# Output stages of a two-layer decoder trunk: turning activation rows by DMA transposes of f16 halves in place of TensorE transposes

## What is computed

```
h = RMSNorm(x) ; p = h @ w_in          # 3328 columns: heads of group A and of group B
A = sliding-window attention with sinks (8 query heads, 2 key heads, window 128)
B = retention with per-head decay (4 heads), per-head RMS norm
mixed = concat(silu(g_A) * A, silu(g_B) * B)
x = x + mixed @ w_out                  # 1024 x 1024
```

## Time and profile before

| | us |
|---|---|
| median of 3 runs | 2056.47 (2053.58 to 2058.32) |
| profiled execution, its own time | 2057.81 |
| span of that execution, first to last instruction | 2055.3 |
| O of layer 0, first to last matmul | 883.85 to 1093.5 |
| O of layer 1, first to last matmul | 1866.68 to 2050.9 |
| PE, DVE, ACT busy over the span | 93%, 71%, 38% |

### The profile page before, as it was taken

One profiled execution on the slowest core, in us unless ns is written; L12 is line 12 of the kernel. 1 busy time (PEld: TensorE's weight loads), 2 busy tenths in 40 slices (PEclk: granted clock), 3 DMA queues, 4 the chain that ended last, 5 costly groups with the idle time before them and its releaser, 6 DMA issues.

```text
span 2055.3 us, 38859 instructions
## 1 busy us (share of the span) xinstructions
PE 1915.4 (93%) x12808; PEld 1111.9 (54%) x12808; DVE 1451.5 (71%) x5064; ACT 782.3 (38%) x1977; POOL 67.7 (3%) x108
## 2 busy tenths in 40 slices
PE   2279999999999999999998999999999999999999
PEld 2246565555555555554554655565555555555454
DVE  6548999987665676668874799999766567666342
ACT  5634555552222223234653445555322221223121
POOL 4000000010000000030001000000000000000000
PEclk9589999999999999999999999999999999999999
DMA  8631000021100210053333000001210021002442
GB/s 277 235 106 28 16 16 10 15 74 60 31 10 10 96 60 10 13 190 115 131 124 123 28 15 11 15 13 34 80 50 10 13 96 60 10 10 91 144 153 92
DMA packets 68283, 137.52 MB, mean 67 GB/s; under 512 B 9808, under 2 KB 40720, under 8 KB 67888
## 3 DMA queue, kind: packets, MB, share of 16 engines
q1 hardware_dynamic: 58464, 100.76, 14.3%
q0 software_dynamic: 9728, 35.66, 5.1%
HBM read 97.27 MB, written 49.68 MB: 71 GB/s over the span
## 4 chain that ended last, share of the span: by engine, by line
PE 40%; DVE 12%; issue 2%; ACT 2%; DMA 1%; DVEq 0%; SPq 0%; ACTq 0%
PE PA L461 16%; PE PB L461 15%; DVE r L997 2%; DVE r L973 1%; DVE mix L1037 1%; DVE w_mx L830 1%; PE OB L626 1%; PE S L607 1%; PE TK L596 1%; ACT r L1541 1%; PE S L642 1%; PE X L648 1%; PE OB L633 1%; PE X L559 1%; PE TK L648 1%
## 5 line engine op out<-in xcount | busy, mean ns | idle before, releaser
L461 PE MATMUL PA<-w_a,hT 128*128 128x512 f16 (+1 forms) x1920 | 403.1, 360 | 8.1 <-DVE land L951 8.1
L461 PE MATMUL PB<-w_a,hT 128*128 128x512 f16 (+1 forms) x1920 | 402.1, 359 | 0.0
L461 PEld LDWEIGHTS PA<-w_a,hT 128*128 (+1 forms) x1920 | 185.3, 99 | 181.3 <-DVE land L951 9.0
L461 PEld LDWEIGHTS PB<-w_a,hT 128*128 (+1 forms) x1920 | 184.6, 98 | 178.1 <-issue 10.5
L1541 ACT ACTIVATE r<-r,nm,unqk 128x256 f32<-128x256 f32 x256 | 150.5, 589 | 116.2 <-DVE sd L1005 116.2
L1599 ACT ACTIVATE r<-OB 128x128 f32<-128x128 f32 (+1 forms) x136 | 36.3, 272 | 386.5 <-PE S L642 360.1
L461 PE MATMUL PA<-w_b,hT 128*128 128x512 f16 x768 | 179.3, 384 | 0.0
L461 PE MATMUL PA<-w_b,r 128*128 128x512 f16 x768 | 177.1, 382 | 1.9 <-DVE r L1191 1.6
L461 PE MATMUL PB<-w_b,hT 128*128 128x512 f16 x768 | 176.3, 379 | 0.0
L461 PE MATMUL PB<-w_b,r 128*128 128x512 f16 x768 | 173.8, 379 | 0.0
L1086 DVE TENSOR_TENSOR r<-S,t_dec 128x256 f32<-128x256 f32 x64 | 27.1, 424 | 153.6 <-PE S L607 153.5
(11 more groups left out here) (239 smaller groups left out, 3036.1 us busy)
## 6 DMA issues: line engine op xcount, KB each, us to landing
out<-r SPq DMA_DIRECT2D x40, 512.0 KB, 2.6
r<-mixed SPq DMA_DIRECT2D x32, 512.0 KB, 4.5
r<-out SPq DMA_DIRECT2D x32, 512.0 KB, 3.5
r<-in_x_prompt SPq DMA_DIRECT2D x16, 512.0 KB, 6.1
w_b<-in_w_in POOLq DMA_DIRECT2D x16, 512.0 KB, 9.0
mixed<-mix SPq DMA_DIRECT2D x32, 256.0 KB, 2.0
w_a<-in_w_in POOLq DMA_DIRECT2D x16, 512.0 KB, 8.1
mixed<-mix SPq DMA_DIRECT2D x64, 128.0 KB, 1.8
```

Of the source, the lines that this page charges most:

```text
L461: last = nc.tensor.matmul(out[0:s.rows, 0:n], lhs, w16(ph, k, p, wpart), start=(k == 0 and part == 0 and wpart == 0), stop=(k == KT - 1 an ...
```

## The change

In O, the rows stay with tokens on partitions until they are f16 halves, and the halves are turned by a DMA. ACT `o_mhi` now writes hi = f16(mixed row times `minv`) to `mh`, one instruction; DVE `o_mlo` writes lo = (row times `minv`) − hi beside it, one instruction; SP `mixed_T` issues one `dma_start_transpose` of the [tokens, 2048] f16 rows to `mT`, and PE waits for its landing (`o_tm`). In layer 0, ACT `x_high` and DVE `x_low` do the same to the new x, to one buffer `xh` in `land`, and SP `h_T` transposes it to `hT` (`h_lo`, now counted in 16s). The transposes of the prologue stay on PE. Both DMAs and all loads and stores of x and mixed are issued on SP's queue. `h_squares` writes its unneeded squares to `land`, and layer 1's first tile waits (DVE and ACT) until all 17 `h_T` have landed.

The order in the step changed too:

```diff
+                def o_step(s, k=None):              # DVE
+                    if not (s - 1).sample:
+                        o_add(L, s - 1, 1)
+                    if not (s.fixed and s.c == 1):
+                        v.wait_ge(dve_piece, piece("O", L, old, 1) + 2)
+                        o_unscale(L, s)
+                    if far:
+                        o_scale(L, s + 2)
...
+                    if k is not None:
+                        w_low(L + 1, "A", k, 0)
                     if not last:
                         h_rstd(L, s - 1)
+                    if far:
+                        o_mlo(L, s + 2)
+                    if not last:
+                        x_low(L, s - 1)
+                    if not s.sample:
+                        o_add(L, s, 0)
                     if k is not None:
                         w_low(L + 1, "A", k, 1)
-                    if not last:
-                        h_lo_part(L, s - 1)
-                    o_add(L, s, 1)
-                    if k is not None:
                         w_low(L + 1, "A", k, 2)
```

```diff
+                def mixed_T(s):                     # SP
+                    if s.fixed and s.c == 1:
+                        alone(sp, b_o, bn("B1", L, F) + 1)
+                    elif not s.sample and not (s.fixed and s.c == 0):
+                        old = T0 if s.fixed and s.c == SAMPLE_AT + 1 else T1 if s.fixed and s.c == SAMPLE_AT + 2 else s - 2
+                        alone(sp, pe_piece, piece("O", L, old, 1) + 1)
+                    alone(sp, o_lo, L * STEPS + s.v + 1)
+                    sp.dma_start_transpose(mT_of(s), mh_of(s)[0:s.rows, :, :].rearrange("p e n -> p (e n)")
+                                           ).then_inc(o_tm[s.par], 16)
+                def h_T(s):
+                    alone(sp, x_lo, L * STEPS + s.v + 1)
+                    sp.dma_start_transpose(hT[:, :, :, hcols(s)].rearrange("p e k t -> p (e k) t"),
+                                           xh[0:s.rows, :, :].rearrange("p e n -> p (e n)")).then_inc(h_lo, 16)
+            def x_high(L, s):                       # ACT
+                act.wait_ge(h_rs, hn(L, s) + 1)
+                act.wait_ge(h_lo, 16 * hn(L, s))
+                A.activation(xh[0:r, 0, :], xt_[0:r, b, :], ACT.Copy, scale=xy[0:r, b:b + 1]).then_inc(x_hi, 1)
```

More of the change, by code:

```diff
@@ L1403, in o_step @@
                     if not last:
                         h_rstd(L, s - 1)
-                    if not (s.fixed and s.c == STEPS - 1):
-                        v.wait_ge(dve_piece, piece("O", L, s - 1, 1) + 2)
-                        o_unscale(L, s + 1)
-                        o_mlo(L, s + 1)
-                    if k is not None:
-                        w_low(L + 1, "A", k, 0)
-                    if not (s.fixed and s.c >= STEPS - 2):
-                        o_scale(L, s + 2)
-                    o_add(L, s, 0)
+                    if far:
+                        o_mlo(L, s + 2)
@@ L1424, in layer @@
-                o_unscale(L, T2)
-                o_mlo(L, T2)
-                if not last:
-                    h_rstd(L, T1)
-                o_scale(L, mid(4))
-                o_add(L, S, 0)
-                o_add(L, S, 1)
-                v.wait_ge(dve_piece, piece("O", L, S, 1) + 2)
-                o_unscale(L, mid(4))
-                o_mlo(L, mid(4))
-                if not last:
-                    h_lo_part(L, T1)
-                    h_rstd(L, S)
-                o_scale(L, mid(5))
@@ L1442, in layer @@
                     v.wait_ge(ch_l, L * 2 + 3)
-                for c in range(3, CV0):
-                    if c > 3:
-                        o_step(mid(c), early=c == 4)
-                    if not last and c < 6:
+                for c in range(1, CV0):
+                    o_step(mid(c))
+                    if not last and 3 <= c < 6:
                         for q in ((0, 1), (2, 3, 4), (5, 6, 7))[c - 3]:
@@ L1765, in o_step @@
                         h_squares(L, s - 1)
-                    if not (s.fixed and s.c == STEPS - 1):
-                        o_mhi(L, s + 1)
+                    if not (s.fixed and s.c >= STEPS - 2):
+                        o_mhi(L, s + 2)
                     if k is not None:
```

315 lines of the change are left out of this document (141 added, 174 removed).

## The result

| | before | changed kernel |
|---|---|---|
| time, median of 6 runs | 2054.56 us (2052.52 to 2058.32) | 2063.6 us (2062.27 to 2064.69) |
| ratio to before, 95% interval | | 1.0042 (1.0030 to 1.0053) |
| profiled execution, its span | 2057.81, 2055.3 | 2063.55, 2061.6 |
| O of layer 0, of layer 1 (first to last product) | 209.7, 184.2 | 225.5, 175.9 |

The change makes the kernel 0.4% slower; the forecast was 0.6% faster. Layer 1 gains 8 us, layer 0 loses 16. The page shows first that the work did leave TensorE: 408 instructions fewer than in the earlier trace rows, 48 × 8 and the 24 short ones. VectorE has what it had.

The account below looks back on a forecast made before the run. PE, busy 93% of the span, was taken as the bound. Layer 0 +1.3, into layer 1 −0.5 and layer 1 −12.2 gave −11.4 from 2057.81: 2046.4 profiled, 2045 as a time; range 2036 to 2140, forecast's own 2036 to 2049.

Parts of the forecast that it names:

- What leaves PE: Both output stages: 48 groups of 8 transposes at 0.87 us plus about 1.3, 43 us of PE, 2.1%.
- T in steady steps: DMA transpose from issue to landing, 512 KB: taken as 6 us, hidden in steady steps of both layers.
- The issue on SP: Taken as 0.34 us; as a rival, up to 3 us costs 8 of the gain, 6 us gives +32; no separate chance.
- The round of DVE and ACT: Layer 0's weight-splitting steps: 13.1 us with 3.2 waiting for ACT, against 12.11 before; seven steps +6.9.
- Start of layer 0: Layer 0's output stage up to `mid(4)`: 15.5 us of stalls replace 5 of transposes and 9 of old waits, +1.3.
- the crowd: About 886 to 918, where the next weights load: a transpose there takes 6 us more, landing after 12.
- Layer 1: Layer 1's output stage: 16 × 0.87 + 0.5 = 14.4 less a stall of about 2 at T1, −12.2 us.
- Into layer 1: From layer 0's last piece to layer 1's first tile: DVE ends sooner, but the last `h_T` must land, −0.5 us.
- Near no change: Rival: T of 7 to 8.5, longer stalls, layer 1 loses half its gain; −4 to +8, about 2058; chance 0.09.
- The single `xh` buffer: Rival, layer 0's steps: T + 2.5 passes 13.1 at T = 10.6; +83, 2140 at T = 12.3; chance 0.22 with slow starts.
- All of PE's time comes back: Rival: the DVE and ACT round does not bind, only start stalls stay; −43, 2013 us; chance 0.07.
- Much slower: Rival: T of 20 to 27.8, layer 0's step over 22 us, layer 1's over 15; over 2300 us; chance 0.16.

Follow-up runs that it names:

- no_h_transposes: Changed kernel with the 17 DMA transposes of layer 1's new h rows left out: 2058.19 us, ratio 1.0014 to the kernel before.
- split_order: Changed kernel with w_high 0, w_high 1 (ScalarE) and w_low 1 (VectorE) moved earlier in layer 0's weight-splitting steps: 2035.23 us, ratio 0.9914.
- all_three: Changed kernel with the later weight load, the new ScalarE/VectorE order in splitting steps, and T2's transpose earlier on SP: 2029.35 us, ratio 0.9877.
- paced: `all_three` with layer 1's first weight load cut in three, behind the landed transposes of T1, T2 and mid(4): 2028.21 us, ratio 0.9872.
- w_later: Changed kernel with the load of layer 1's first weights started only when T1's transposed mixed rows have landed: 2056.97 us, ratio 1.0004.
- paced_early: `paced` with the load in four parts, mid(4)'s transpose earlier on SP and its low half before the sample tile's sums: 2028.63 us, ratio 0.9876.
- early_sums: `paced_early` with a step's first `o_add` put ahead of `x_low` where no weights are split: 2030.73 us, ratio 0.9881.

## Why the prediction was wrong

- **What leaves PE: right.** 8 transposes cost 0.87 us a step, layer 1's steps went from 11.24 to 10.36, and 408 instructions went.
- **T in steady steps: right side, a bit careful.** T was taken as 6 and is 4.3 in the median; it hides, as said. The estimate of about 4 from the Trainium skill ("DMA: Bandwidth & Descriptors", Latency and other measured facts) was the nearer one. The other rule quoted from the Trainium skill, 1309 ns a block ("VectorE: DVE Perf Modes", The three transpose paths), taken one after another, would have been 21 us; the trace doesn't agree with reading it so, since 16 blocks land in 4.3 us.
- **The issue on SP: mis-sized by six, without effect in steady steps.** Taken as 0.34 us, it is 2.1 in the median for mixed rows and 1.8 for h rows. The rival text had said what 3 us an issue would cost (8 of the gain); `no_h_transposes` shows that in the changed kernel's rounds it costs nothing.
- **The round of DVE and ACT: the mechanism right, the size 0.45 us short.** 13.1 was forecast, 13.55 measured, with both waits at the places named (2.20 and 1.25 against 3.2 together). The seven steps came to +10.1 in place of +6.9. `split_order` shows it: 26 to 28 us less for moving three calls.
- **Start of layer 0: the step that failed**, 13.2 of the 17.7 us of error. The sum said that T1's transpose takes 12 us in the crowd (6 + 6) and that `mid(4)` begins 1.3 us later. The landing is 15.2. The stalls are 10.33 + 4.19 + 3.84 + 1.96 = 20.3 where 15.5 were forecast: T1's is 10.33 for 8, T2's 3.84 for 5.6, and `mid(4)`'s 1.96 for 1.9, though for its transpose and not for T2's `o_add`. The 4.19 among them was not seen at all: the stores of the state are in the same crowd, and ACT, then DVE, wait for them. And the lower clock after each long stall, which the sum left out, adds 1.3 + 2.7 + 1.7 = 5.7 up to `mid(4)`. (The kernel before lost 1.7 there too, 12 matmuls in 4.44 us for 2.75, but within what the sum took off as old waits.) The 4.8, the 5.7 and about 1 us from before O make 11.5 of the 13.2; the rest isn't laid to a single row. The sum for T1's issue is loose by under 1 us: O starts at 883.85 in the rows, not 883.0, and the terms give 889.97, not 890.4.
- **Layer 1: −8.3 for −12.2.** T1 does not wait, but T2 does, 3.43 us with 1.7 of lower clock: its transpose is queued behind another tile's x load. The stage had 15 full groups of transposes to lose and not 16, since T0's run before O begins; 15 × 0.87 + 0.5 less these 5.1 gives 8.4. In `all_three`, with that order mended, layer 1's O has no stall.
- **Into layer 1: −2.0 for −0.5**, inside what single profiles carry.
- **The rivals.** "Near no change", −4 to +8, comes nearest to the measured +9, but by T of 7 to 8.5, which isn't the cause: it would have been right by luck. The single `xh` buffer does not bind the changed kernel. "All of PE's time comes back" failed on the two orders and the load; `paced` and `all_three`, which leave nothing out and beat both kernels, stand at 0.987 and 0.988, and what is between them and 2013 is the start of layer 0. "Much slower" is out.
- **The error in the weighing.** All rivals hung on one unknown, T in the steady state, and the crowd was a fixed 6 us on one transpose in each of them. The sign hung on the start and on a round that was known to be longer than before. A gain of 11 us out of 43, what was left after two named losses of 15.5 us stalls and 6.9 us of rounds, deserved no 0.53.

What stays open: why one transpose beside a weight load is held up on SP for 11 to 12 us whether 5.2 MB are loading (`w_later`, `all_three`) or quarters of 1.3 MB are sent out (`paced_early`, `early_sums`), and why T1's in the changed kernel is issued in 3.64 us and then lands late. Taking the load's bytes away ends it, with its 24 transfers still sent out. Whether it waits for the load's packets on the DMA engines or for the memory, no run here tells apart.

## What to carry to other kernels

Moving transposes from TensorE to DMA pays where TensorE is the late one and the DMA engines have room, as in layer 1; a stage that also loads weights needs its transposes out of that load's way, or keeps some on TensorE. Before such a move is made, write the new round of the helping engines call by call: a copy that TensorE's transposes used to separate now stands next to its partner, and the pair waits. When a wait goes away, look what the thing waited for will meet next: the load was moved three times (later, in three parts, in four), and the stall moved with it. The change itself was not lost: with the orders mended and the load later it is 1.2% faster than the kernel before (`all_three`).

## What the runs showed of the hardware

- A DMA transpose of 512 KB goes in some 2080 packets, 250 bytes each: packets went from 68283 to 169750 for 48 full transposes and three of sample rows (a quarter each), (169750 − 68283) / 48.75. It is costly on the DMA engines: in layer 1 the share of the stage went from 0.36 × 184.19 = 66.3 us to 0.63 × 175.88 = 110.8. 15 full transposes and the one of sample rows are issued in that stretch, 15.25 in all, so one takes 2.9 us of all 16 engines; in layer 0, with twice as many, the share went from 86.0 to 187.2, 3.3 each. Stores and loads of the same size, three a step, take 66.3 / 17 / 3 = 1.3 us.
- Its issue holds the queue of SP: 1.2 us for 32 rows, 1.3 to 2.1 in layer 1's steady steps, up to 3.75 in layer 0 of the changed kernel, 11 to 12 for one beside a later weight load. The last one of layer 0, beside the load of B0's weights, took 7.8 to 9.7, and landed after 12.3 to 14.1, in all nine kernels with h transposes.
- What moves beside a transpose and a weight load at once suffers alike: a store of 64 KB took 18.0 us, a median of 5.0 beside the load alone (kernel before) and 3.2 with the load put later (`w_later`), and the engines moved 126 GB/s at a share of 1.22, 335 at 1.05 without the transpose.
- The granted clock was at 1.2 GHz (0.50 to 0.52) in the long idle stretches, and the group of 24 behind one took 6.6 to 8.2 us in place of 5.34; behind shorter ones it did so too (7.04 after 1.96 us and after 3.05) or did not (5.35 after 1.33 us and, later in the stage, after 3.04). It costs time only where PE is the late engine: in the 13.55 us rounds it did not. It also fell once in either layer with no idle time ahead, at a place where the two kernels do the same and before has 1.00; this is the row of the changed kernel's layer 0 (busy by engine, then PEclk, DMA share, GB/s), and it takes 1.7 us:

```profile
720.00:725.00 5.00, 5.00 (x21) 2.31 (x20) 4.48 (x21) 0.60 (x1) 0.00 (x0) 0.73 0.44 128
```
